# Re-timing the delta-rule preparation: table clears between tiles, gate products two tiles ahead, the first inverse group behind tile 6, the second in parts between merges

## The reference

```python
gam = jnp.cumsum(g, axis=-1)
decay = jnp.exp(jnp.where(incl, gam[..., :, None] - gam[..., None, :], -jnp.inf))
kb = k * beta[..., None]
a = jnp.where(strict, jnp.einsum("bhncd,bhnsd->bhncs", kb, k) * decay, 0.0)
rhs = jnp.concatenate([v * beta[..., None], kb * jnp.exp(gam)[..., None]], axis=-1)
sol = lax.linalg.triangular_solve(a, rhs, left_side=True, lower=True, unit_diagonal=True)
u, w = sol[..., :dv], sol[..., dv:]
...
p = jnp.einsum("bhncd,bhnsd->bhncs", q, k) * decay
xs += [p, q * jnp.exp(gam)[..., None]]
```

## Time and profile before

| | us |
|---|---|
| median of 3 runs | 1771.34 (1769.95 to 1773.77) |
| profiled execution | 1775.21 |
| its span | 1773.3 |
| block of the delta-rule preparation in it | 654 to 880 |
| busy over the span: PE / DVE / ACT / POOL | 1493.1 / 727.4 / 378.2 / 390.6 |

### The profile page before, as it was taken

How to read it: one execution, slowest core, us unless ns; L and a number is a source line. 1 busy time by engine, 2 the same in 40 slices (tenths; PEclk the granted TensorE clock), 3 DMA queues, 4 the chain that set the end, 5 groups by cost and what they waited for, 6 DMA issues and landing times. The chain is left out here.

```text
span 1773.3 us, 22024 instructions
## 1 busy us (share of the span) xinstructions
PE 1493.1 (84%) x8736; PEld 803.4 (45%) x8736; DVE 727.4 (41%) x1137; ACT 378.2 (21%) x755; POOL 390.6 (22%) x413
## 2 busy tenths in 40 slices
PE   3999999998899875429899985499999999999960
PEld 0644566475454433218795442244444444443420
DVE  2267585744656634726576225311111111111116
ACT  3201111124444443204422111011111111111102
POOL 0000002435666656414481000000000000000003
PEclk9999999999999986659989997699999999999985
DMA  9533200009900000131112002999999999999937
GB/s 361 214 119 143 83 0 1 0 1 345 347 1 1 1 9 22 38 53 27 40 61 108 0 4 113 421 400 427 427 428 427 427 427 427 427 427 428 363 118 296
DMA packets 111199, 352.96 MB, mean 199 GB/s; under 512 B 41806, under 2 KB 75757, under 8 KB 94580
## 3 DMA queue, kind: packets, MB, share of 16 engines
q1 hardware_dynamic: 101162, 315.91, 45.4%
q0 software_dynamic: 6048, 22.02, 3.2%
q10 hardware_dynamic: 3888, 13.63, 1.9%
HBM read 295.69 MB, written 55.84 MB: 198 GB/s over the span
## 5 line engine op out<-in xcount | busy, mean ns | idle before, releaser
L2538 PE MATMUL psum<-arena 128*64 128x512 f32 (+1 forms) x1680 | 531.2, 599 | 21.8 <-DMA arena<-in_expert_w_down 10.2
L2538 PEld LDWEIGHTS psum<-arena 128*64 128x64 f32 (+1 forms) x1680 | 204.8, 161 | 312.1 <-issue 298.4
L804 PE MATMUL psum<-arena 128*128 128x512 f32 (+1 forms) x416 | 166.2, 556 | 1.0 <-DVE arena L256 1.0
L899 POOL TENSOR_TENSOR arena<-arena 128x512 f32<-128x512 f32 x112 | 145.4, 1321 | 89.1 <-DVE arena L917 65.8
L2495 DVE TENSOR_TENSOR arena<-arena,psum 128x512 f32<-128x512 f32 x25 | 17.2, 688 | 337.4 <-PE psum L2538 337.4
L2420 POOL DMA_INDIRECT arena<-normed_rows,arena x26 | 24.6, 945 | 568.5 <-PE psum L2530 506.7
L381 DVE TENSOR_REDUCE q_hl<-psum 128x1 fp32r<-128x1280 f32 x64 | 94.6, 1478 | 72.2 <-PE psum L373 72.2
L804 PEld LDWEIGHTS psum<-arena 128*128 128x128 f32 x416 | 78.7, 193 | 88.1 <-issue 80.2
L1970 PE MATMUL psum<-arena 128*128 128x512 f32 x256 | 110.4, 593 | 1.7 <-ACT arena L1832 0.8
L966 ACT ACTIVATE arena<-psum 128x512 f32<-128x512 f32 x160 | 86.6, 598 | 78.3 <-PE psum L1013 78.2
L2506 DVE SCALAR_TENSOR_TENSOR small<-psum,small,arena 128x512 f32<-128x512 f32 x50 | 35.2, 747 | 152.3 <-PE psum L2538 152.3
(11 more groups left out here) (381 smaller groups left out, 1804.6 us busy)
## 6 DMA issues: line engine op xcount, KB each, us to landing
arena<-in_expert_w_gate SPq DMA_DIRECT2D x35, 2048.0 KB, 28.6
arena<-in_expert_w_up SPq DMA_DIRECT2D x35, 2048.0 KB, 26.5
arena<-in_expert_w_down SPq DMA_DIRECT2D x35, 2048.0 KB, 22.7
expert_out<-small SPq DMA_DIRECT2D x1, 29696.0 KB, 89.7
arena<-in_mod_w SPq DMA_DIRECT2D x24, 1024.0 KB, 6.6
expert_out<-small ACTq DMA_DIRECT2D x25, 512.0 KB, 10.2
arena<-in_w_in SPq DMA_DIRECT2D x2, 3072.0 KB, 10.8
arena<-in_x SPq DMA_DIRECT2D x8, 512.0 KB, 13.8
```

The costliest lines, as they stand in the source:

```text
L804: last = nc.tensor.matmul(b[:, 0:nt], w[:, k, i * P:(i + 1) * P], hT[:, k, t0:t0 + nt], **flags)
L899: nc.gpsimd.tensor_tensor(acc[:, p % 2, b], acc[:, p % 2, b], pT[:, order2(p, j, b) % 8], ALU.add).then_inc(s2_add, 1)
L2538: last = nc.tensor.matmul(psum[r, bank, :], lhs[:, k, r], w.rearrange("p (k f) -> p k f", k=n)[:, k, cols], start=k == 0, stop=k == n - 1)
```

## The change

- POOL no longer clears the two tables ahead of the loop. It clears a fifth of each (two tiles) behind `masked_decay` of tiles 0 to 4. The diagonal of `sysXT` gets a semaphore of its own, `s3_unit`.
- `gU` has two buffers, and the span products alternate between banks 6 and 7. DVE forms `prefix(t + 2)` and `normalised(t + 2)` between `spans(t + 1)` and `lower(t)`; PE issues the span product of t+2 ahead of the Gram products of t. For tile 1 it waits until ACT has read the totals out of bank 7.
- `base(0)` comes behind tile 6 instead of 7. SP gathers the diagonals of tile 5 in the same iteration as its store, and does `spread(0)` behind the store of tile 6 instead of 8.
- Of the 16 loads of group 0, SP issues the 8 of `XT_all` and ACT the 8 of `X_all`, behind its work for tile 7; ACT waits for the confirmation of the stores first. Group 1's loads are all on SP as before.
- `base(1)` is cut into four parts (steps 1 to 4, 5 to 8, 9 to 12, 13 to 15 with the copy), behind the outputs of merges 0 to 3.

```diff
-        gU, decay = at(131, 2, NH, HD), at(133, 2, 8, HD)
+        gU, decay = (at(131, 2, NH, HD), at(171, 2, NH, HD)), at(133, 2, 8, HD)
...
+        def inverse_in(eng, g, n):
+
+            s0, ns = SLOTS[g]
+            v = (XT_all, X_all)[n]
+            for m in range(8):
+                rows = bass.AP(inv_h, ((n * 8 + m) * TA + 2 * s0) * 8 * 256, [[16, 16], [256, 16 * ns], [1, 16]])
+                j = m % 4 * 16
+                eng.dma_start(v[16 * m:16 * m + 16, 2 * s0:2 * s0 + 2 * ns, :, j:j + 16].rearrange("p t a j -> p (t a) j"),
+                              rows).then_inc(s3_inv[g], 16)
...
                 if g == 0:
-                    sp.wait_ge(s3_clear, 1)
-                for n, v in enumerate((XT_all, X_all)):
-                    for m in range(8):
...
+                    sp.wait_ge(s3_clear, 5)
+                inverse_in(sp, g, 0)
+                if g == 1:
+                    inverse_in(sp, g, 1)
 
             for t in range(TA):
                 sp.wait_ge(s3_L, t + 1)
                 sp.dma_start(low_dram[t], Ln_all[:, t].rearrange("p a n -> p (a n)")).then_inc(s3_low[t % 2], 16)
-                if t:
+                if t and t != LAST_TILE[0]:
                     collect(t - 1)
-                if t == 8:
+                if t == LAST_TILE[0] - 1:
+                    collect(t)
+                if t == LAST_TILE[0]:
                     spread(0)
             collect(TA - 1)
             spread(1)
...
-            nc.gpsimd.memset(XT_all, 0.0)
-            nc.gpsimd.memset(X_all, 0.0).then_inc(s3_clear, 1)
...
                 masked_decay(t)
+                if t < TA // 2:
+                    nc.gpsimd.memset(XT_all[:, 2 * t:2 * t + 2], 0.0)
+                    nc.gpsimd.memset(X_all[:, 2 * t:2 * t + 2], 0.0).then_inc(s3_clear, 1)
...
             for t in range(1, TA):
                 transposed(t)
                 decayed(t)
+                if t == LAST_TILE[0] + 1:
+                    act.wait_ge(s3_back[0], 16 * 4 * SLOTS[0][1])
+                    act.wait_ge(s3_clear, 5)
+                    inverse_in(act, 0, 1)
...
-            def base(g):
+            def base(g, steps):
 
                 s0, ns = SLOTS[g]
-                dve.wait_ge(s3_sys[g], 16 * 8 * 2 * ns)
-                if g == 0:
-                    dve.wait_ge(s3_clear, 1)
-                else:
-                    dve.wait_ge(s3_back[0], 16 * 4 * SLOTS[0][1])
-                for i in range(1, 16):
+                if steps[0] == 1:
+                    dve.wait_ge(s3_sys[g], 16 * 8 * 2 * ns)
+                    if g == 0:
+                        dve.wait_ge(s3_unit, 1)
+                    else:
+                        dve.wait_ge(s3_back[0], 16 * 4 * SLOTS[0][1])
+                for i in steps:
...
             normalised(0)
             prefix(0)
+            prefix(1)
             spans(0)
             normalised(1)
             for t in range(TA):
                 if t + 1 < TA:
-                    prefix(t + 1)
                     spans(t + 1)
+                if t + 2 < TA:
+                    prefix(t + 2)
+                    normalised(t + 2)
                 lower(t)
-                if t + 2 < TA:
-                    normalised(t + 2)
                 if lat(t):
                     scores(t)
...
-                if t == 7:
-                    base(0)
-            base(1)
+                if t == LAST_TILE[0]:
+                    base(0, range(1, 16))
...
                 outputs(t)
+                if t < 4:
+                    base(1, range(1 + 4 * t, min(5 + 4 * t, 16)))
...
             def spans(t):
                 pe.wait_ge(s3_gU, t + 1)
-                if t:
-                    pe.wait_ge(s3_E, t)
-                nc.tensor.matmul(psum[:, 6, :], m_same, gU.rearrange("p d h n -> p (d h n)"), start=True, stop=True
+                if t == 1:
+                    pe.wait_ge(s3_gl, 4)
+                if t >= 2:
+                    pe.wait_ge(s3_E, t - 1)
+                nc.tensor.matmul(psum[:, 6 + t % 2, :], m_same, gU[t % 2].rearrange("p d h n -> p (d h n)"), start=True, stop=True
                                  ).then_inc(s3_gb, 1)
...
             for t in range(TA):
                 if t + 1 < TA:
                     transposed(t + 1)
-                    spans(t + 1)
+                if t == 0:
+                    spans(1)
+                if t + 2 < TA:
+                    spans(t + 2)
                 gram(t)
```

More of the change, by code:

```diff
@@ L1146, in sems @@
             return (sem("s3_" + n) for n in names.split())
-        s3_cst, s3_row, s3_one, s3_clear = sems("cst row one clear")
+        s3_cst, s3_row, s3_one, s3_unit, s3_clear = sems("cst row one unit clear")
         s3_tr, s3_tra, s3_trd = sems("tr tra trd")
@@ L1221, in spread @@
                 if g == 0:
-                    sp.wait_ge(s3_clear, 1)
-                for n, v in enumerate((XT_all, X_all)):
-                    for m in range(8):
-                        rows = bass.AP(inv_h, ((n * 8 + m) * TA + 2 * s0) * 8 * 256, [[16, 16], [256, 16 * ns], [1, 16]])
-                        j = m % 4 * 16
-                        sp.dma_start(v[16 * m:16 * m + 16, 2 * s0:2 * s0 + 2 * ns, :, j:j + 16].rearrange("p t a j -> p (t a) j"),
-                                     rows).then_inc(s3_inv[g], 16)
+                    sp.wait_ge(s3_clear, 5)
+                inverse_in(sp, g, 0)
+                if g == 1:
+                    inverse_in(sp, g, 1)
             for t in range(TA):
@@ L1252, in _ @@
             pool.wait_ge(s3_one, 2)
-            nc.gpsimd.memset(sysXT.rearrange("p s i j -> p s (i j)")[:, :, 0:256:17], 1.0)
-            nc.gpsimd.memset(XT_all, 0.0)
-            nc.gpsimd.memset(X_all, 0.0).then_inc(s3_clear, 1)
+            nc.gpsimd.memset(sysXT.rearrange("p s i j -> p s (i j)")[:, :, 0:256:17], 1.0).then_inc(s3_unit, 1)
             pool.wait_ge(s3_cst, 48)
@@ L1462, in prefix @@
                 dve.wait_ge(s3_g, 1)
-                if t:
-                    dve.wait_ge(s3_gb, t)
-                nc.vector.tensor_tensor(gU, m_inc.unsqueeze(2).broadcast_to([P, 2, NH, HD]),
+                if t >= 2:
+                    dve.wait_ge(s3_gb, t - 1)
+                nc.vector.tensor_tensor(gU[t % 2], m_inc.unsqueeze(2).broadcast_to([P, 2, NH, HD]),
                                         gx[:, t].unsqueeze(3).broadcast_to([P, 2, NH, HD]), ALU.mult).then_inc(s3_gU, 1)
@@ L1473, in spans @@
                         dve.wait_ge(s3_dinc, t - 1 - NCT)
-                nc.vector.tensor_tensor(decay[:, t % 2], bank(6), wide(gam[:, t]), ALU.subtract).then_inc(s3_E, 1)
+                nc.vector.tensor_tensor(decay[:, t % 2], bank(6 + t % 2), wide(gam[:, t]), ALU.subtract).then_inc(s3_E, 1)
             def normalised(t):
@@ L1511, in base @@
                     chain(nc.vector.tensor_reduce(sysXT[:, 0:ns, 0:i, i], part, AX.X, ALU.add))
-                nc.vector.tensor_copy(sysX[:, 0:ns].rearrange("p s i j -> p s j i"), sysXT[:, 0:ns]).then_inc(s3_base[g], 1)
+                if steps[-1] == 15:
+                    nc.vector.tensor_copy(sysX[:, 0:ns].rearrange("p s i j -> p s j i"), sysXT[:, 0:ns]).then_inc(s3_base[g], 1)
             dve.wait_ge(s3_stdn, 1)
```

## The result

The changed kernel took 1766.14 us in the median of 20 runs (1762.5 to 1769.91), the kernel before 1773.36 us in 20 runs (1767.2 to 1778.41). The ratio is 0.9963 with a 95% interval of 0.9953 to 0.9972; six more runs of it, with a second profile, gave 0.9958 (0.9944 to 0.9972). That is 6.5 to 7.4 us faster where 14.4 were forecast; the median lies 4 us above the forecast of 1750 to 1762 us and just above the bounds of 1748 to 1766.

The account below looks back on a forecast made before the run. Bound seen in the delta-rule stage: POOL's head, the loop's ring of waits, two inverse groups. Sum: -12 to group one's end, -18.7 to the third step, +16.3 in the merges, -14.4: 1757 us; forecast 1750 to 1762 (0.70), bounds 1748 to 1766.

Parts of the forecast that it names:

- step 4: Return of group one, loads split over SP and ACT: ACT issues for 4.4 us, first merge at +23 behind group one.
- step 6: Second group in four parts among the merges: last part at +38 from tile 0's third step, 14 us stall before tile 6.
- Step 1: Start of the block: without POOL's two big memsets key scaling starts 5.8 us earlier; 2.3 us arrive at tile 0's Gram product.
- Step 2: Tile loop: 5.6 us per latent tile and 5.2 per context tile instead of 6.28; Gram of tile 5 at 714.1.
- the ring: The tile loop's cycle of waits: subtraction, gate product, span product, Gram, lower; POOL's own 5.3 us a tile just covered.
- Step 3: First inverse group a tile earlier: new 2.6 us wait for gathers, 14.8 us of work, DVE free 12 us earlier, at 740.
- rival A: Return of group one: ACT's eight loads take 8.8 to 11.4 us instead of 4.4; 1761 to 1764 us; chance 0.14.
- Step 5: First merge: 6.6 us to the third step of tile 0, at 769.6 instead of 800.32, 30.7 us earlier.
- Rival B: Merges, broken up by parts and stall, run at the loop's clock of 0.68: slower, 1782 us; chance 0.05.
- Rival C: Stall before tile 6 shorter with loads at 0.32 us each, and loop at full clock: 1747 to 1750 us; chance 0.06.
- rival D: Loop stays at 6.3 us a tile through POOL's memsets, group one awaited longer, ACT's loads slow: 1765 to 1770 us; chance 0.05.

## Why the prediction was off

The sign was right, and each wait stood where the prediction put it; the gain was half of what was forecast. Three terms failed. The way of group one (step 4) was put at 4.4 us of issue on ACT, which took 6.4. The second group in parts (step 6) was priced without POOL's work beside it, 12.4 us for parts that took 16.5. And the profile of before, from which the gain was counted, had a loop that was 5 us longer than in the second profile of the same kernel.

**Step 1** held. Counted from the first normalisation (673.07 before, 675.98 after) the key scaling came at +0.9 and the Gram product of tile 0 at +13.5, where +13.8 was worked out. All of it lay 2.5 us later, because the token transposes ahead of it ran at half clock in this execution: 3 us from the start of the block the granted clock was 0.50 for 3 us, and then 0.54, where it was 0.99 and 1.00 before.

**Step 2**, the ring, was worked out as 27.2 us for five periods; they took 24.5 and 25.1 us in the two profiles. The clock was nearer to full than assumed (0.92 and 0.85 from 691 to 715 us), and POOL, at 5.25 us a tile without a pause, was a bound close to the 5.3 worked out. The -4 for a loop all at full clock did not come. What failed is the other side of the difference: the 31.4 us of before were taken from one execution, and the second has 26.5. The 6.28 us of the prediction were the mean of a loop that ran at both levels, 4.9 us a latent tile at full clock and up to 7.0 at half; such a ring can't be read off one profile. With means of both profiles the gain at the end of group one is 11.8 us, near the forecast 12, but only because errors cancel: the loop of before was quicker than taken by 2.5 us and that of the changed kernel by 2.4. Counted from the reciprocal the gain is 14.0; the start of the changed kernel, 2.2 us longer, took back the rest.

**Step 3** held: forecast 725.1 for the start of group one and 14.8 us for its length, measured 723.27 and 14.8. The landing took 1.2 us behind the last gather instead of 2.9 (the row from which that was taken gives 2.7), so the new wait was 0.9 us and not 2.6.

**Step 4** failed in its size, by 2 us. SP's pace of 0.55 us a load was put on ACT; with both queues at work ACT took 6.41 us for 8 loads (0.80 each) and SP 5.83 (0.73). That is rival A in less than half its size, and the sign "ACT issues for much more than 4.4 us". The prediction held against it that SP was never slowed below 0.55 a load; its own have 11.34 us for 16, which is 0.71. The median issue of a load was 604 ns on ACT, the longest 1337, where SP alone had 486 and 529 at most in the run without ACT's loads. The first merge came at +25.2 instead of +23. The trace put the last wait where the step said, on POOL's mask behind ACT.

**Step 5** held: 6.7 us from the first merge to the third step of tile 0, worked out 6.6. That the third step came at 769.85, where 769.6 was worked out, is luck: group one ended 2 us sooner than 740, and ACT held the merge 2 us longer.

**Step 6** failed in its price for the parts. It took 11.4 us from a stretch in which POOL was idle and added 1 us; the parts took 16.5 us, and the run with POOL's products cut shows 4.1 us of that to be the wait for POOL. The prediction had the two rows for it, 1.09 against 0.68 for the gate product and 0.56 against 0.16 for the first product of a group, used them for the loop and for group one, and not for the one place where the change puts DVE's small products beside POOL's work. From the third step of tile 0 the last part ended at +41.1 instead of +38. The return took 16.9 us instead of 18.1, the stall was 11.2 us, 14 forecast. Behind it 42.4 us remained (39.1 before, 40 forecast): with tile 6 waiting, its first products, ACT's copy and the second products run one behind the other, at a granted clock of 0.58 from 828 to 835 us, and the clock fell again for the last tile, to 0.72 from 864 to 870. Between them, from 834 to 864, it was 1.00.

Summed, by the means of two profiles each: +0.2 us to the end of group one, +2.6 on the way to the merges and +2.7 in them, which makes -8.9 for the block out of the forecast -14.4; some 2 us more lie in the rest of the kernel. Rival B fell: it needed a clock of 0.81 or less in the merges to turn the sign and put 0.68, and the clock was 0.88 from 769 to 870 us with the stall in it. That is just under the 0.9 that the prediction named as a sign of being wrong. Rival C fell, the stall was 11.2 us and the loads went at 0.52 each. The time lies in the range of rival D (1765 to 1770), but not by its mechanism: the memsets did bound the ring, at 5.25 us and not 6.3, and the gain of the loop was there.

The larger miss is one of weighing. By its own numbers the prediction had the moved groups give 18.7 us and take 16.3, beside what the move of group one gave in the -12, and called the whole a gain of 14; it didn't ask what the loop would do alone. That is 0.992, and the moved groups are worth nothing or less: 212.0 us for the block with the loop alone, 214.8 with all of the change.

Two readings of the profile of before were off and carried no number. Its PE row has a slice with 2 tenths too, the 18th, from 753 to 798 us, where PE waits for the first group. And the clock falls to 5 in that slice, not to 6 (the page's row of the granted clock has 8, 6, 6, 5, 9, 9 for slices 15 to 20).

## What to carry to other kernels

An inversion that goes out through memory has a way home that is longer than its own work (here 17 us behind the 11.4 us of the inversion): work out when its consumer wants it before cutting the work into parts, because the last part sets the time of return. Before a transfer is split over two queues, look which queue has something behind it that others wait for, and give the free queue the work that the full one is holding up. And price small VectorE products by the stretch into which they are moved, with GpSimd's work beside them, not by the one from which they come.

## What the runs showed of the hardware that was not expected

- Beside POOL's tensor_tensor, DVE's products of two SBUF operands wait however small they are: 1.01 us for 8 elements a partition, 1.06 for 50, against 0.17 and 0.21 alone; both end within 0.1 us of the end of POOL's instruction. Reductions with one operand take the same time in both (327 ns in the mean), and beside a memset on POOL a product of 512 elements took 0.68 us, as alone.
- Sixteen loads of 64-byte runs for the first group took 8.8 us to issue on one queue, with no other DMA beside them. On two queues eight each took 5.8 and 6.4 us, with the DMA engines at 0.88 over 740 to 765 us. The Trainium skill (DMA: Bandwidth & Descriptors, Issuing engines are not separate DMA queues) says that a second issuing engine saves only issue time; of that, 2.4 us were saved here, the median time from issue to landing went from 2.8 us to 5.6, and 4.1 us were lost on ACT.
- The same loop of the same kernel took 26.5 us and 31.4 us for five tiles in two executions. In the shorter one the granted clock was 1.00 (2.4 GHz) from 694 to 714 us; in the longer one it was 0.50 (1.2 GHz) until 704 and changed between the two levels after that the earlier trace rows.
- The token transposes at the start of the block took 18.3 to 18.5 us up to the reciprocal in all five profiles of kernels with the clears at POOL's head (before twice, clears at the head twice, gate products alone), and 20.0 to 20.9 in six of nine with the clears between the tiles, 18.3 in the other three. The transposes are the same. From 3 to 6 us behind the start of the block the granted clock was 0.99 and 0.91 in the two profiles of before (18.4 and 18.3 us), and 0.50 in both of the changed kernel (20.9 and 20.2 us). Why it rose later is open.
